# Triangular inverses of the DeltaNet chunks: 32x32 block transposes, smaller last levels, masks and scalings on other engines

## The reference, cut to what matters

```
k_beta = k * beta[..., None]
decay  = jnp.exp(jnp.where(tri, g[..., :, None] - g[..., None, :], -jnp.inf))
lower  = jnp.where(tri_strict, einsum('bhncd,bhnsd->bhncs', k_beta, k) * decay, 0.0)
rhs    = concatenate([v * beta[..., None], k_beta * jnp.exp(g)[..., None]], axis=-1)
sol    = triangular_solve(lower + eye, rhs, left_side=True, lower=True, unit_diagonal=True)
u, w   = sol[..., :Dv], sol[..., Dv:]
# then, chunk after chunk, with a 128x128 state for each head:
v_new  = u_c - w_c @ state
o_c    = q_c @ state + intra_c @ v_new
state  = state * exp(gl_c) + k_c.T @ v_new
```

## Time and profile before

| what | value |
|---|---|
| median of 3 runs | 1419.29 us |
| the profiled execution | 1421.1 us |
| its span, first to last instruction | 1419.3 us |
| mean granted TensorE clock | 0.95 |
| PE busy | 1248.3 us (88%) |
| DVE busy | 524.0 us (37%) |
| ACT busy | 222.9 us (16%) |
| POOL busy | 304.9 us (21%) |
| DMA | 446.07 MB, mean 314 GB/s |

### The profile page before, as it was taken

How to read it: one execution, slowest core, us unless ns; L and a number is a source line. 1 busy time by engine, 2 the same in 40 slices (tenths; PEclk the granted TensorE clock), 3 DMA queues, 4 the chain that set the end, 5 groups by cost and what they waited for, 6 DMA issues and landing times.

```text
span 1419.3 us, 31113 instructions
## 1 busy us (share of the span) xinstructions
PE 1248.3 (88%) x12281; PEld 614.0 (43%) x12282; DVE 524.0 (37%) x1230; ACT 222.9 (16%) x432; POOL 304.9 (21%) x411
## 2 busy tenths in 40 slices
PE   7989987999879989797979899997988767799897
PEld 6865447984554433232324333332333322244333
DVE  1237777432353333232323233332333232233322
ACT  3135643441200000000000000000000000000000
POOL 3000014000042222222222222222222212222223
PEclk9999999999879999999989999999999988899999
DMA  6211012019569999999999999999999999999991
GB/s 192 71 60 60 30 60 60 2 45 365 210 270 406 411 418 417 416 416 417 416 417 418 420 363 391 412 408 416 419 419 416 420 416 424 419 418 359 417 420 37
DMA packets 62020, 446.07 MB, mean 314 GB/s; under 512 B 11585, under 2 KB 32009, under 8 KB 37409
## 3 DMA queue, kind: packets, MB, share of 16 engines
q1 hardware_dynamic: 46384, 428.77, 72.9%
q0 software_dynamic: 15600, 16.81, 5.5%
HBM read 435.11 MB, written 14.81 MB: 317 GB/s over the span
## 4 chain that ended last, share of the span: by engine, by line
PE 42%; DMA 42%; DVE 8%; issue 5%; POOL 1%; ACT 1%; SPq 1%; POOLq 1%; DVEq 0%; ACTq 0%
DMA XG<-hn_scratch,IDXC 22%; DMA BDN<-in_expert_b_down 18%; PE PS L579 18%; PE PS L909 14%; PE PS L922 5%; PE PSC L579 3%; DVE XT L1232 2%; POOL IDXC L358 1%; DVE GU L1241 1%; PE PS L784 1%; DMA W<-in_w_in 1%; SPq L193 1%; DVE BDN L1257 0%; PE PS L718 0%; DVEq L1278 0%
## 5 line engine op out<-in xcount | busy, mean ns | idle before, releaser
L909 PE MATMUL PS<-W,XT 128*32 128x512 f32 x5184 | 600.4, 616 | 119.3 <-DVE XT L1232 115.0
L909 PEld LDWEIGHTS PS<-W,XT 128*32 128x32 f32 x5184 | 170.0, 113 | 509.6 <-issue 395.2
L922 PE MATMUL PS<-W,AT 128*32 128x256 f32 x5184 | 294.7, 379 | 1.2 <-DVE AT L1252 1.2
L579 PE MATMUL PS<-W 128*128 128x512 f32 (+6 forms) x1068 | 275.7, 416 | 4.8 <-DVE W L1171 1.9
L922 PEld LDWEIGHTS PS<-W,AT 128*32 128x32 f32 x5184 | 170.8, 110 | 144.4 <-issue 47.6
L579 PEld LDWEIGHTS PS<-W 128*128 128x128 f32 (+1 forms) x1068 | 174.5, 198 | 86.4 <-issue 71.9
L1241 DVE TENSOR_TENSOR GU<-PS,BGU 128x512 f32<-128x512 f32 x81 | 56.0, 691 | 349.8 <-PE PS L909 346.3
L376 POOL DMA_INDIRECT out<-Y,IDXS x81 | 130.4, 1610 | 101.9 <-ACT Y L568 95.1
L568 ACT ACTIVATE Y<-SIG,ident 128x256 f32<-128x256 f32 x81 | 41.1, 508 | 638.9 <-DMA out<-Y,IDXS 619.2
L361 POOL DMA_INDIRECT XG<-hn_scratch,IDXC x82 | 87.6, 1068 | 73.8 <-POOL IDXC L358 67.8
L372 POOL COPY IDXS<-IDX 128x1 uint32 (+1 forms) x81 | 14.9, 184 | 382.6 <-DMA out<-Y,IDXS 382.5
(11 more groups left out here) (228 smaller groups left out, 615.0 us busy)
## 6 DMA issues: line engine op xcount, KB each, us to landing
W<-in_expert_w_gate_up SPq DMA_DIRECT2D x128, 2048.0 KB, 23.0
W<-in_expert_w_down SPq DMA_DIRECT2D x64, 2048.0 KB, 26.3
W<-in_w_in SPq DMA_DIRECT2D x9, 1024.0 KB, 6.5
W<-in_x SPq DMA_DIRECT2D x8, 512.0 KB, 4.8
W<-in_w_in SPq DMA_DIRECT2D x2, 1040.0 KB, 5.6
W<-in_w_out SPq DMA_DIRECT2D x1, 2048.0 KB, 7.6
W<-in_w_out SPq DMA_DIRECT2D x2, 1024.0 KB, 10.0
out<-W SPq DMA_DIRECT2D x4, 512.0 KB, 11.3
```

The lines of the kernel that those rows point to most:

```text
L579: return pe.matmul(o, l, r, start=st, stop=sp_)
L909: last = pe.matmul(GPS[32 * j:32 * j + 32, :].rearrange("p (g n) -> p g n", g=2), XT[:, 32 * k:32 * k + 32], rhs, start=(k == 0), stop=(k ...
L922: last = pe.matmul(DPS[32 * j:32 * j + 32, :], AT[:, 32 * k:32 * k + 32], DNW[p][:, k, j * QW:(j + 1) * QW], start=(k == 0), stop=(k == KD ...
```

## The change

It does five things. (1) In levels 2 to 16, U is made from T by VectorE's transpose, which turns each 32x32 block in place: up to this size, T is zero outside the 32x32 blocks on the diagonal. TensorE's transpose of T and ScalarE's copy of it go, at all levels. (2) Level 32 works on the two nonzero corners of 32x32 only (8 matmuls of 32x32 a product), level 64 on the one of 64x64 (4 matmuls a product, and the second product gives the corner of U directly); VectorE writes the corners with a factor -1. (3) The CT masks of levels 2 to 16 are made on GpSimd, and VB moves behind the first four masks in the loop. (4) KB = KH * beta is made on ScalarE, as 4 copies with a per-partition scale. (5) VectorE no longer subtracts GC; instead exp on ScalarE takes -GC (a new tile NGC) as its bias, as 4 operations of 128 columns. The semaphore `kq_scaled` is split into `kh_ready`, `kb_ready` and `qn_ready`.

```diff
# SP, ahead of the WO0 transfers
-            sp.wait_ge(S_("kq_scaled"), 3 * NT)
+            sp.wait_ge(S_("qn_ready"), NT)
             sp.wait_ge(S_("vb_ready"), NT)
# GpSimd
+            def below_diagonal(c, lv):
+                g.tensor_tensor(h4(B[c]["CT"]), h4(B[c]["LT"]), bm(MSK[lv + 1], HD), ALU.mult).then_inc(S_("ct"), 1)
             for c in range(NT):
-                g.tensor_tensor(h4(B[c]["VB"]), VTM[:, c, :, :], bc(BETA[:, 4 * c:4 * c + 4], P), ALU.mult).then_inc(S_("vb_ready"), 1)
+                g.wait_ge(S_("u_init"), c + 1)
+                below_diagonal(c, 0)
+            for m in range(3 * NT):
+                g.wait_ge(S_("p1_ps"), m + 1)
+                below_diagonal(m % NT, m // NT + 1)
+                if m < NT:
+                    g.tensor_tensor(h4(B[m]["VB"]), ...).then_inc(S_("vb_ready"), 1)
# ScalarE, prepare(c)
+                a.wait_ge(S_("kh_ready"), c + 1)
+                for h in range(HD):
+                    ins = a.activation(b["KB"][:, hs], b["KH"][:, hs], ACT.Copy, scale=BETA[:, 4 * c + h:4 * c + h + 1])
+                ins.then_inc(S_("kb_ready"), 1)
                 a.wait_ge(S_("dsub"), c + 1)
-                a.activation(b["DEC"], b["DEC"], ACT.Exp).then_inc(S_("decay"), 1)
+                for h in range(HD):
+                    ins = a.activation(b["DEC"][:, hs], b["DEC"][:, hs], ACT.Exp, bias=NGC[:, 4 * c + h:4 * c + h + 1])
+                ins.then_inc(S_("decay"), 1)
# TensorE, the level loop
+            def corners(lv):
+                return [(b, b + 32, 32) for b in (0, 64)] if lv == 4 else [(0, 64, 64)]
...
+                    else:
+                        for h in range(HD):
+                            for at, to, s in corners(lv):
+                                last = pe.matmul(bank[to:to + s, h * s:h * s + s], b["LT"][at:at + s, h * P + to:h * P + to + s],
+                                                 b["T"][at:at + s, h * P + at:h * P + at + s], start=True, stop=True,
+                                                 tile_position=(at, to), skip_group_check=True)
...
-                if m >= 2:
-                    n = m - 2
-                    pe.wait_ge(S_("t_upd"), n + 1)
...
-                        last = pe.transpose(PS[7 - 6 * (n % 2)][:, hs], B[n % NT]["T"][:, hs], ident[:, :])
-                    last.then_inc(S_("tt_ps"), 1)
# VectorE, scaled(c), decayed(c)
-                tt(h4(b["KB"]), h4(b["KH"]), bc(BETA[:, hs], P), ALU.mult).then_inc(S_("kq_scaled"), 1)
-                link(tt(h4(b["DEC"]), h4(AO), bc(GC[:, hs], P), ALU.subtract))
-                tt(h4(b["DEC"]), h4(b["DEC"]), bm(NEGM, HD), ALU.add).then_inc(S_("dsub"), 1)
+                tt(h4(b["DEC"]), h4(AO), bm(NEGM, HD), ALU.add).then_inc(S_("dsub"), 1)
-                tt(h4(b["CT"]), h4(b["LT"]), bm(MSK[1], HD), ALU.mult).then_inc(S_("ct"), 1)
# VectorE, the level loop
+                if lv < 4:
+                    tt(even(b["T"], lv), even(b["T"], lv), compact(bank, lv), ALU.subtract).then_inc(S_("t_upd"), 1)
+                    v.wait_ge(S_("t_upd"), m + 1)
+                    v.transpose(b["U"], b["T"]).then_inc(S_("u_upd"), 1)
+                elif lv == 4:
...
+                        ins = ts(corner, bank[to:to + 32, 0:HD * 32].rearrange("p (h n) -> p h n", h=HD), -1.0, None, ALU.mult)
...
+                        ins = v.transpose(h4(b["U"])[at:at + 32, :, to:to + 32], h4(b["T"])[to:to + 32, :, at:at + 32])
+                    ins.then_inc(S_("u_upd"), 1)
+                else:
+                    ts(h4(b["U"])[0:64, :, 64:P], bank[0:64, 0:HD * 64].rearrange("p (h n) -> p h n", h=HD), -1.0, None, ALU.mult).then_inc(S_("u_upd"), 1)
```

More of the change, by code:

```diff
@@ L78, in hybrid_block @@
         GC, GLC = small(248, 16), small(264, 16)
+        NGC = small(200, 16)
         EG, EGD, EGL = small(280, 16), small(296, 16), small(312, 16)
@@ L502, in _ @@
             t0_copy(1)
[L503 to L506, removed]
+            for m in range(len(LEVELS) * NT):
+                lv, bank, p1 = m // NT, PS[4 + m % 2], B[m % NT]["P1"]
+                a.wait_ge(S_("p1_ps"), m + 1)
+                if lv < 4:
+                    a.activation(p1[:, 0:HD * 64], bank[:, 0:HD * 64], ACT.Copy).then_inc(S_("p1_ready"), 1)
+                elif lv == 4:
+                    a.activation(p1[:, 0:HD * 32], bank[:, 0:HD * 32], ACT.Copy).then_inc(S_("p1_ready"), 1)
+                else:
+                    a.activation(p1[64:P, 0:HD * 64], bank[64:P, 0:HD * 64], ACT.Copy).then_inc(S_("p1_ready"), 1)
                 if m < 2:
                     t0_copy(m + 2)
[L509 to L511 removed]
             def uw_copies(c):
@@ L750, in _ @@
             STEPS = len(LEVELS) * NT
-            for m in range(STEPS + 2):
+            def corners(lv):
+                return [(b, b + 32, 32) for b in (0, 64)] if lv == 4 else [(0, 64, 64)]
+            for m in range(STEPS + 1):
                 if m < STEPS:
-                    b = B[m % NT]
-                    pe.wait_ge(S_("ct"), m + 1)
+                    b, lv, bank = B[m % NT], m // NT, PS[4 + m % 2]
                     if m >= NT:
@@ L769, in _ @@
                         pe.wait_ge(S_("t_ready"), 3)
-                    for h in range(HD):
-                        last = mm(PS[6 - 6 * (n % 2)][:, h * 64:h * 64 + 64], b["U"][:, h * P:(h + 1) * P], b["P1"][:, h * 64:h * 64 + 64], True, True)
+                    if n >= 2:
+                        if n - 2 < 5 * NT:
+                            pe.wait_ge(S_("t_upd"), n - 1)
+                        else:
+                            pe.wait_ge(S_("u_upd"), n - 1)
+                    if lv < 4:
+                        for h in range(HD):
+                            last = mm(bank[:, h * 64:h * 64 + 64], b["U"][:, h * P:(h + 1) * P], b["P1"][:, h * 64:h * 64 + 64], True, True)
+                    elif lv == 4:
+                        for h in range(HD):
+                            for at, to, s in corners(lv):
+                                last = pe.matmul(bank[to:to + s, h * s:h * s + s], b["U"][to:to + s, h * P + to:h * P + to + s],
+                                                 b["P1"][to:to + s, h * s:h * s + s], start=True, stop=True,
+                                                 tile_position=(to, to), skip_group_check=True)
+                    else:
+                        for h in range(HD):
+                            last = pe.matmul(bank[0:64, h * 64:h * 64 + 64], b["P1"][64:P, h * 64:h * 64 + 64],
+                                             b["U"][64:P, h * P + 64:h * P + P], start=True, stop=True,
+                                             tile_position=(64, 0), skip_group_check=True)
                     last.then_inc(S_("p2_ps"), 1)
@@ L1093, in _ @@
                     link(v.tensor_copy(GC, AO[:, 0:16]))
+                    link(ts(NGC, AO[:, 0:16], -1.0, None, ALU.mult))
                     v.tensor_copy(GLC, AO[:, 16:32]).then_inc(S_("dn_vec"), 1)
```

54 lines of the change are left out of this document (29 added, 25 removed).

## The result

| | median | lowest to highest | runs |
|---|---|---|---|
| before | 1421.01 us | 1414.48 to 1423.78 | 17 |
| after | 1411.61 us | 1407.35 to 1416.33 | 17 |

The changed kernel takes 0.9937 of the time of before, 95% interval 0.9924 to 0.995: faster by 9.4 us, about half of the 17.6 us forecast, and 0.6 us outside the range (1394 to 1411). Its profiled execution took 1411.66 us, with a span of 1409.9 and a clock of 0.951.

What follows compares the result with a forecast made beforehand. PE was taken to bound the level loop and weight transfers the experts. The loop falling from 53.6 to 38.2 us (15.4 gained) plus 2.2 ahead of it made 17.6 us: 1402 us, range 1394 to 1411.

Steps and rivals of the forecast that it cites:

- The step that failed: From the chain ahead of 293 us to the end: time saved there comes off the end, 17.6 us in all.
- Rival D: Expert phase: the weight stream is held by something the shift leaves in place, hiding the gain; 1419 us, chance 0.03.
- Levels 2 to 16: First 16 steps of the level loop: PE binds at 1.73 us a step, 27.7 us in all.
- the transpose of 128x512: DVE's block transpose in the level loop: 1.16 us, scaled from 0.654 for 128x256, bounds 0.684 and 1.31.
- rival A: Level loop: DVE's transposes wait for GpSimd, 15.5 us lost and 2 left; 1417 us, chance 0.06.
- Levels 32 and 64 and the tail: End of the level loop: 5.8 us for level 32, 4.0 for level 64, 0.7 for the tail.
- level 4 (s = 32): Level 32: 1.45 us a step; the PSUM bank rule against it would keep products at 0.86 us, 1.1 us more.
- Rival B: Level loop: without its transposes PE waits, the clock falls to 1.2 GHz, ending slower; 1433 us, chance 0.04.
- Ahead of the loop: Preparation before the levels: DVE loses operations, ACT gains some; 2.2 us gained, bounds -2 and +5.6.
- ScalarE's four operations: Preparation, per chunk: KB as four copies takes 1.25 us, and the exp grows from 0.63 to 1.25 us.
- WO0: Its transfers, behind the later VB, are issued at about 247 us instead of 235.80, at no cost.

Runs made afterwards that it cites:

- a93: The changed kernel with 93 more TensorE instructions (empty waits), making its code as long as before: 1405.32 us, ratio 0.9893.
- w1: The changed kernel with one unread full-size dummy product per step of levels 32 and 64, code kept as long as before: 1402.81 us, ratio 0.9875.
- kd93: The changed kernel, code as long as before, with KB and the decay difference back on VectorE: 1406.63 us, ratio 0.9898.
- a40: The changed kernel with 40 more TensorE instructions of empty waits: 1411.12 us, ratio 0.9933.
- a170: The changed kernel with 170 more TensorE instructions of empty waits: 1416.38 us, ratio 0.997.
- o93: The changed kernel, code as long as before, with levels 32 and 64 done as in the kernel before: 1409.73 us, ratio 0.9932.
- w2: The changed kernel with two dummy products per step of levels 32 and 64 and 29 instructions of empty waits: 1406.24 us, ratio 0.9897.

## Why the prediction was wrong

**The step that failed** is the end of its first paragraph: "a microsecond taken from the chain ahead of 293 us should come off the end, if nothing in between waits for something that does not move". Something did: TensorE's code. The chain was shortened by 16.45 us where the forecast had 17.6, and a93 shows 15.4 of them at the end. After has 9.4. The missing 6.0 us arose between blocks 0 and 3 of the experts (37.52 us for 31.00 in a93): 1.0 us ahead of block 1 and 3.9 ahead of block 2, both starts standing 3.7 us behind a packet of instructions, and 1.7 in block 2, whose clock had fallen to 0.50 for 3.4 us. The hole in the weights that follows keeps the loss to the end. Rival D had the right place (the stream "held by something that the shift leaves where it is") with a chance of 0.03, but as a hold on the whole gain; no case of the prediction has a cost for the place of the program's own code.

The Trainium skill (Runtime: NRT & Kernel Launch, "Instruction fetch mechanics") says that code comes in blocks of 16 KiB or 256 instructions, read ahead in sequence, and that a taken branch out of what is loaded forces a DMA read before execution goes on. The packets of 16 KB in queue 8 and the 3.6 to 3.7 us from their start to the next product agree. The runs show that the place of the code decides. That a taken branch is what makes the packet start so late is argued from that page and wasn't tried.

**Levels 2 to 16: right, with the reason mis-sized.** 28.65 us from the first product to the first of level 32 (27.7 forecast). The chain:

```profile
235.70 1.08 PE PSC L599 x8
236.77 0.44 PE PS L764 x4
237.21 0.84 PE PSC L599 x8
238.05 0.89 PE PS L599 x8
...
241.12 0.90 PE PSC L599 x8
242.02 0.89 PE PS L599 x8
```

PE binds, as forecast, but a step is 0.90 + 0.89 = 1.79 and not 1.73 (the 0.84 was that of a product behind a transpose), and two transposes that make the first U (0.44 each) were not counted. DVE isn't just under PE but far: the transpose of 128x512 took 0.711 us, near the lower bound (0.684), not 1.16:

```profile
L1158 DVE STREAM_TRANSPOSE W<-W 128x512 f32<-128x512 f32 x14 | 10.0, 711 | 0.5
L336 POOL TENSOR_TENSOR W<-W 128x512 f32<-128x512 f32 x13 | 16.3, 1273 | 2.6 <-DVE W L1110 1.6 <-PE PSC L599 1.0
```

The row it was scaled from the earlier trace rows still has 654 ns for half the columns in the experts (line 1297). That one reads its source with the columns interleaved (line 163), the new one in order; whether this is the reason wasn't tried. All 16 transposes, most of them beside the masks and VB and the last ones behind the last mask (257.66 us), took 0.711 or 0.712 us, so rival A falls. VectorE was slowed ahead of the loop only, where both operands are in SBUF: line 1110 took 1.65 us beside a mask of 1.72, and 0.69 without:

```profile
228.96 1.65 DVE L1110 TENSOR_TENSOR W<-ident,W 128x512 f32<-128x512 f32 x1
232.83 0.69 DVE L1110 TENSOR_TENSOR W<-ident,W 128x512 f32<-128x512 f32 x1
...
228.34 1.72 POOL L336 TENSOR_TENSOR W<-W 128x512 f32<-128x512 f32 x1
```

**Levels 32 and 64 and the tail: right in size** (9.8 + 0.7 = 10.5 forecast, 264.35 to 274.81 = 10.46 measured), which is luck in part: the measured time holds a fallen clock that the forecast didn't have. At level 32 DVE sets the pace: its pairs of scalings start at 266.99, 268.29 and 269.59 us, 1.30 apart for the 1.45 forecast, with no idle time between but the hand-over of 0.02 to 0.04 us. PE was busy beside it, at half the clock from 267.76 on.

```profile
L1169 DVE STREAM_TRANSPOSE W<-W 32x128 f32<-32x128 f32 x8 | 2.4, 303 | 0.2
L1162 DVE TENSOR_SCALAR W<-PS 32x128 f32<-32x128 f32 x8 | 2.3, 290 | 0.3
```

By the Trainium skill's rule that the prediction set against its level 4 (s = 32) (TensorEngine Tiling (Array Packing), "Gotcha 1: PSUM Pressure"), as the prediction priced it, a product stays at 0.86 us. The 16 instructions of the first product took 0.37, at clock 1.00:

```profile
264.35 0.37 PE PSC L787 x16
```

That is under the forecast's own lower value of 0.43, so the 1.1 us that this rule would have added did not come. Whether the tiles waited for each other within these 0.37 us the rows don't show.

**Rival B came, behind the 16 steps it was written for.** The clock was 1.00 in all of them and 0.50 (1.2 GHz of 2.4) from 267.76 to 278.00 us, so that its mean is 0.77 over level 32 and 0.50 over level 64. It fell in level 32, where PE had been busy 2.70 of 3.41 us:

```profile
264.35:267.76 3.41, 2.70 (x105) 2.40 (x106) 2.97 (x7) 1.11 (x4) 0.00 (x0) 1.00 0.02 5
267.76:270.70 2.94, 2.94 (x50) 2.69 (x52) 2.70 (x10) 0.38 (x1) 0.00 (x0) 0.50 0.00 0
```

It stayed down with PE busy 2.94 of 2.94 us there and 4.11 of 4.11 in level 64, so idle time of PE isn't what kept it down. Whether the fall itself came from the gaps or from the size of the products isn't separated: the full-size dummy products of w1 also fill the gaps (PE busy 6.50 of 6.50 us), and the clock stays at 1.00 there. The next product behind the levels took 3.52 us against 1.79 in the earlier trace rows, 1.7 lost.

```profile
273.23 1.58 PE PS L815 x14
274.81 3.52 PE PS L599 x16
```

**Ahead of the loop: right in sign, larger.** The first product came 3.7 us earlier (235.70), 2.2 forecast. ScalarE's four operations are 1.27 us (forecast 1.25):

```profile
219.55 1.27 ACT L461 ACTIVATE W<-W,SM 128x128 f32<-128x128 f32 x4
220.72 1.27 ACT L466 ACTIVATE W<-W,SM 128x128 f32<-128x128 f32 x4
```

By kd93, the two moves to ScalarE are worth 1.4 us of the preparation. The clock in 215 to 235.7 us is 1.00, for 0.85 in 215 to 237 of before; that this gave the rest is likely and not shown. A sign of it: the changed preparation takes 34.8 us in a93, a40, a170 and o93, where the clock stood at 0.50 for 3.4 us of it, and 36.8 in after, w1 and w2, where it stood at 0.50 for 6.8 to 10.2 us. WO0 went at 246.77 (247 forecast) and held up nothing.

The sum: 3.7 (front) + 14.5 (levels, 39.1 for 53.6) - 1.7 (clock) = 16.5 at the first weights, less 6.0 (place of the code, with the clock that fell behind it) and about 1 that also a93 loses = 9.4. The last 1 us has no cause shown.

## What to carry to other kernels

A hand-written loop that reads its code from memory has a place in it: before a shorter prologue is judged, look for an "issue" wait of some us at the same spot of the loop's first rounds and for queue-8 packets at that time, and compare with a version padded back to the old length. A gain that is a rigid shift is only rigid if the stage behind it starts in the same state, and here a stall in the stage paced by DMA kept its whole price. A stage of small products can be quick for itself and leave a lower clock to what comes next; here one full-size dummy product a step held it.

## What the runs showed of the hardware

- Reading one 16 KB block of TensorE's code while the weights use the DMA at 0.9 or more took 3.6 to 3.7 us from the packet's start to the next product; the wait open ahead of block 2 was 0.16 to 5.05 us by the place of the code, and blocks 0 to 3 took 6.5 to 7.8 us longer at the worst place, 1.7 to 3 us of it by a clock of 0.50 behind the wait.
- Waits on completed semaphores had a price: 163 instructions of them behind the first convolution unit put the first weights back by 11.9 us, 93 by nothing that could be told (a93), 170 by 8.4. The pause of TensorE behind them was 2.92 us with 93, 10.44 with 163 and 11.19 with 170, which makes 0.107 us for each instruction more; an estimate from this is that the first 7 us or so ran while the 16 products ahead of them (7.13 us) were still being worked off.
- VectorE's transposes: 128x512 in 0.711 us, 32x128 in 0.303 us; GpSimd beside them made no difference.
